# Moving the normed x 64 bytes along in SBUF, in a float32 decoder trunk on one core

## What is computed

```
h = rms_norm(x, pre_mix_norm[l])
proj = h @ w_in[l]                       # 2048 x 5648: q, k, v, z, xbc, dt
mix = concat(attention(q,k,v), ssd(xbc, dt, z))
x = x + rms_norm(mix @ w_out[l], post_mix_norm[l])          # 2048 x 2048
h = rms_norm(x, pre_mlp_norm[l])
x = x + rms_norm(square(relu(h @ w_up[l])) @ w_down[l], post_mlp_norm[l])   # 2048 x 8192, 8192 x 2048
```

## The kernel before, in words

| tile | first byte | its remainder by 128 |
|---|---|---|
| raw, w_hi, w_lo, x_sb | 16512, 32896, 49280, 65664 | 0 |
| a_hi, a_lo | 82048, 98432 | 0 |
| u_hi, u_lo, ybuf | 114816, 131200, 147584 | 0 |
| xbcT, x_tok, v_tok, zg, b_tok, convr | 163968 and on | 0 |
| wk, cbm | 206016, 214208 | 64 |
| wdt_both | 216256 | 64 |
| ident, tri, low | 218688, 219200, 219712 | 64 |

## Time and profile before

### The profile page before, as it was taken

One profiled execution on the slowest core, in us unless ns is written; L12 is line 12 of the kernel. 1 busy time (PEld: TensorE's weight loads), 2 busy tenths in 40 slices (PEclk: granted clock), 3 DMA queues, 4 the chain that ended last, 5 costly groups with the idle time before them and its releaser, 6 DMA issues.

```text
span 2248.1 us, 39497 instructions
## 1 busy us (share of the span) xinstructions
PE 2216.5 (99%) x14282; PEld 2023.7 (90%) x14282; DVE 1319.9 (59%) x1528; ACT 1016.3 (45%) x1280; POOL 109.9 (5%) x112
## 2 busy tenths in 40 slices
PE   8999999999999999999999999999999999999997
PEld 8999888998998998898899988889989989988986
DVE  6777465655555455555578775657554545554555
ACT  5443464543444344344454435545434434443443
POOL 2141000000000000000001410000000000000000
PEclk9999999999999999999999999999999999999999
DMA  6555556556656656655645555655666566556565
GB/s 204 152 170 157 161 188 198 177 179 200 189 180 192 190 179 193 190 184 187 193 125 166 166 161 151 198 185 182 190 192 186 173 201 188 184 189 193 176 194 163
DMA packets 208448, 406.21 MB, mean 181 GB/s; under 512 B 12540, under 2 KB 12820, under 8 KB 207828
## 3 DMA queue, kind: packets, MB, share of 16 engines
q1 hardware_dynamic: 206660, 398.04, 57.3%
q10 hardware_dynamic: 992, 4.78, 0.6%
q0 software_dynamic: 688, 1.90, 0.4%
HBM read 402.58 MB, written 2.10 MB: 180 GB/s over the span
## 4 chain that ended last, share of the span: by engine, by line
issue 71%; PE 26%; DVE 1%; ACT 0%; POOL 0%; DMA 0%; DVEq 0%; POOLq 0%; ACTq 0%
PE acc L734 5%; PE acc L737 5%; PE acc L736 5%; PE acc L699 3%; PE acc L701 3%; PE acc L700 3%; PE M L838 1%; PE M L751 1%; DVE x_sb L1111 0%; PE M L859 0%; DVE xbcT L1177 0%; DMA wk<-in_ssd_out_norm 0%; PE M L879 0%; POOL st L393 0%; DVE w_lo L1028 0%
## 5 line engine op out<-in xcount | busy, mean ns | idle before, releaser
L1028 DVE TENSOR_TENSOR w_lo<-raw,w_hi 128x1024 fp32r<-128x1024 f32 x755 | 927.7, 1235 | 793.4 <-ACT w_hi L462 790.1
L462 ACT ACTIVATE w_hi<-raw 128x1024 fp32r<-128x1024 f32 x755 | 794.5, 1058 | 1026.8 <-PE acc L701 521.6
L734 PE MATMUL acc<-a_hi,w_hi 128*128 128x256 f32 x2912 | 828.4, 284 | 1.8 <-DVE w_lo L1028 1.8
L736 PE MATMUL acc<-a_lo,w_hi 128*128 128x256 f32 x2912 | 823.9, 283 | 0.0
L737 PE MATMUL acc<-a_hi,w_lo 128*128 128x256 f32 x2912 | 823.9, 283 | 0.0
L734 PEld LDWEIGHTS acc<-a_hi,w_hi 128*128 128x128 f32 x2912 | 558.6, 192 | 4.1 <-DVE w_lo L1028 2.7
L736 PEld LDWEIGHTS acc<-a_lo,w_hi 128*128 128x128 f32 x2912 | 558.7, 192 | 1.8 <-issue 1.0
L737 PEld LDWEIGHTS acc<-a_hi,w_lo 128*128 128x128 f32 x2912 | 558.7, 192 | 0.0
L699 PE MATMUL acc<-w_hi,u_hi 128*128 128x512 f32 x1280 | 498.6, 390 | 0.0
L700 PE MATMUL acc<-w_lo,u_hi 128*128 128x512 f32 x1280 | 498.0, 389 | 0.0
L701 PE MATMUL acc<-w_hi,u_lo 128*128 128x512 f32 x1280 | 498.0, 389 | 0.0
(11 more groups left out here) (218 smaller groups left out, 1049.2 us busy)
## 6 DMA issues: line engine op xcount, KB each, us to landing
raw<-in_w_up SPq DMA_DIRECT2D x256, 512.0 KB, 3.7
raw<-in_w_down SPq DMA_DIRECT2D x256, 512.0 KB, 4.5
raw<-in_w_in SPq DMA_DIRECT2D x179, 512.0 KB, 3.8
raw<-in_w_out SPq DMA_DIRECT2D x64, 512.0 KB, 4.6
zg<-in_post_mix_norm ACTq DMA_DIRECT2D x2, 1024.0 KB, 4.6
zg<-in_post_mlp_norm ACTq DMA_DIRECT2D x2, 1024.0 KB, 6.4
out<-x_sb SPq DMA_DIRECT2D x8, 256.0 KB, 2.8
x_sb<-in_x POOLq DMA_DIRECT2D x3, 512.0 KB, 7.3
```

Of the source, the lines that this page charges most:

```text
L462: act.activation(w_hi[:, c % RING], raw[:, c % RING], ACT.Copy).then_inc(sem["hi_ready"], 1)
L734: pe.matmul(o(m), w(w_hi, kk, m), a_hi[:, k], start=(k == 0 and m % 2 == 0), stop=False, skip_group_check=True)
L736: pe.matmul(o(m), w(w_hi, kk, m), a_lo[:, k], start=False, stop=False, skip_group_check=True)
L1028: dve.tensor_tensor(w_lo[:, c % RING], raw[:, c % RING], w_hi[:, c % RING].bitcast(F32), ALU.subtract).then_inc(sem["split_done"], 1)
```

## The change

Two tiles of 64 bytes a partition, which nothing writes or reads, are declared ahead of `a_hi` and behind `a_lo`:

```diff
         x_sb = sb("x_sb", [P, TT, D])
+
+        sb("shift_a", [P, 16])
         a_hi = sb("a_hi", [P, KT, SEQ], F32R)
         a_lo = sb("a_lo", [P, KT, SEQ], F32R)
+        sb("shift_back", [P, 16])
         u_hi = sb("u_hi", [P, KT, SEQ], F32R)
         u_lo = sb("u_lo", [P, KT, SEQ], F32R)
```

## The result

| | before | changed |
|---|---|---|
| median of 5 runs each, us | 2249.82 (2249.32 to 2250.53) | 2258.80 (2258.25 to 2259.72) |
| ratio to before, with its 95% interval | | 1.0041 (1.0029 to 1.0054) |
| span of the profiled execution, us | 2248.1 | 2258.0 |
| forecast, us | | 2189 (2147 to 2220) |

The changed kernel is slower by 0.4%, some 9 us. The forecast was 61 us faster, and its range doesn't hold the result. In the changed kernel all lines behind the new declarations have moved on by 3: L734 is L737, L699 is L702, L1028 is L1031.

What follows compares the result with a forecast made beforehand. TensorE bounds the kernel: matmul count times the distance between starts. Gains of 57.3 (features) and 5.1 (v and z) less 0.4 (dt) and 1.0 (settling) make 61.0 us off 2248.1; with 1.7 us for the median, 2189 us, range 2147 to 2220.

Steps and rivals of the forecast that it cites:

- rival A: All matmuls: no change, the dt projection's 113.3 ns comes from something else; 2249.8 us, chance 12%.
- Rival D: Feature matmuls: slower, 126.7 ns, as the moving operand must begin on a multiple of 128; 2304 us, chance 8%.
- rival B: Feature, v and z matmuls: all of the excess goes, 109 ns, 11 less than now; 2147 us, chance 7%.
- Rival C: Half the gain, 3.3 ns on average: starts don't settle with operands changing between w_hi and w_lo; 2219 us, chance 7%.
- Everything behind them keeps its remainder by 128: Tiles behind the two new ones: the 3,840 matmuls with u stay at 226.7 ns, 0 us.
- the 24 starts are even to the 10 ns of the view: dt projection before: even starts over distances 64, 192, 320, 448 by 512, so only the remainder by 128 seems to matter.
- I take the dt projection's 113.3: Feature chunks, 256 columns: 113.3 ns instead of 120.0, 6.7 ns each, 57.3 us gained.
- My bounds of 109 and 126.7: Feature matmuls: 109 ns from x's transposes below, 126.7 above, as far over 120.0 as the dt projection is under.
- v and z: 768 matmuls of 512 columns, stationary a: the same 6.67 ns less each, 5.1 us gained.
- about 120: dt projection: its two operands now start alike, so 64 matmuls lose 6.67 ns each, 0.4 us.
- the 188 ns that I had named as a sign: Up projection: L734's weight loads at 188 ns in the median would show the forecast right.
- Settling: First few matmuls after other work, roughly 50 places a layer: some 2 us less gain at most, 1 taken.

Runs made afterwards that it cites:

- m1_offsets: Model left out, only TensorE works: 32 equal float32r matmuls per pair of operand offsets; 113.3 to 120.0 ns at 256 columns, 226.7 to 233.5 at 512.
- e2: Kernel before with only u, and all behind it, moved on by 128 bytes; 2272.04 us, ratio 1.0100.
- e1: Changed kernel with u 512 bytes behind its old place instead of 128; 2234.64 us, ratio 0.9934.
- e9: Changed kernel with u 256 bytes behind its old place instead of 128; 2234.76 us, ratio 0.9934.
- m2_grid: m1_offsets with all 64 offset pairs by 32 bytes and eight alternating patterns; distance 0 has 120.0 ns at 256 columns, 226.7 to 227.2 at 512.
- e7: Changed kernel with a moved by 192 bytes instead of 64, and u 256 bytes on; 2218.69 us, ratio 0.9861.
- e8: e7 with two float32 ident matmuls ahead of the first up block of each quarter from the second on; 2200.59 us, ratio 0.9781.
- e3: Kernel before with the weight ring (w_hi, w_lo) moved on by 64 bytes, a and u by 256; 2209.20 us, ratio 0.9820.
- e6: e1 with two float32 ident matmuls ahead of each pair of up blocks from the second quarter on; 2240.36 us, ratio 0.9957.
- e5: Kernel before with ring and u 64 bytes on by 256, plus two ident matmuls ahead of each pair of up blocks from the second quarter; 2216.25 us, ratio 0.9851.

## Why the prediction was wrong

It was right about what bounds the kernel. The time is the count of matmuls times their spacing, the waits stayed (0.1 us among the three of the earlier trace rows), no transfer and no split came late, and the place of the operands does alter the spacing: rival A's world, in which it can't matter, is excluded by m1_offsets. The Trainium skill, page "SBUF — State Buffer", section "Who interferes with whom", gives TensorE's moving operand and its weight load a read port each, independent of each other, and has it wait on no one. The small kernels, with no other engine at work, have 113.3 to 120.0 ns and 226.7 to 234.5 for the same shapes, by place. So the measurement decides against the conclusion that the place can't matter; whether the ports are what depends on each other, no run here shows.

Rival D put a slowdown on the features (126.7 ns), which in fact gained; rival B's 109 ns was seen at no distance. Rival C's small gain is near the 2.2 ns measured, but by another way: it blamed the change between tiles, and the small kernel has the 117.8 with one stationary and one moving tile. The 109 ns that B and D leaned on say little: the earlier trace rows are float32 transposes of 128 columns, not 256, and in the changed kernel, where ident's place turned their distance from +64 to -64, they start 109 ns apart as before. The slowdown came from where no rival looked. These steps failed:

- **"Everything behind them keeps its remainder by 128, so the 3,840 matmuls with u keep their 226.7 ns: 0 us."** They took 233.3 ns, +25 us, the largest term of all. u lies 128 behind its old place, and the period is 256: distance 128 costs 232.1 to 233.5 in the small kernels, e2 shows the loss alone, e1 and e9 undo it. Without it the change is 0.7% faster (e9, 2234.76).
- What it rested on: **"the 24 starts are even to the 10 ns of the view, so only the remainder by 128 seems to matter"**. By 256 the dt projection has distances 64 and 192 in turn, and each of them alone has another value, 113.3 and 117.8. The mix is even at 113.3, in m2_grid too. An even row over a mix doesn't show that its parts are alike.
- **"I take the dt projection's 113.3 ...; only which of the two is off the 128 differs."** It did matter which. The distance is +64 there in half of the matmuls, and -64 in all of the changed features: 117.8 instead of 113.3, a gain of 19.3 us instead of 57.3. But the sign is only a part of the 38 us between: with the other sign alone (e7) the features are at 117.18 on average, 13 us less than the change has. Another 20 us lie between e7 and e8 (114.93), in the state of the six long runs; the last 5 are short runs and first matmuls that stay above 113.3 in e8 too. My bounds of 109 and 126.7 held the 117.8.
- **v and z: "Since the excess was the same at both widths, I take the same 6.67 ns."** The size was nearly right and the sign wrong: +64 at 512 columns is 233.3, 6.6 more, and the term +4.0 us instead of -5.1.
- The dt projection, "about 120", came to 117.5 where its distances are now 128 and 0 in turn; it is worth 0.2 us. The weight loads came to the 188 ns that I had named as a sign, and yet the features didn't come to 113.3: the loads take 188 at 113.3 (e3) and at 117.8, so their length doesn't tell the one from the other. **"Settling"** was priced at 1 us, for the first few matmuls of each run. What stands ahead of a run can matter far more: two small matmuls ahead of each of six runs are the whole of the 18 us between e7 and e8.

By its own terms, the sum was -57.3 - 5.1 + 0.4 + 1.0 = -61.0; measured it was -19.3 + 4.0 + 25.2 + 0.2 = +10.1. Of the 71 us between them, 38 are the spacing at 256 columns, 25 the period, 9 the value at +64 with 512 columns; the rest, the dt projection's 0.2 and the 1.0 for settling, takes 1 off. The 8% for slower stood on rival D alone; the loss came from 3840 matmuls under a term put at nothing, and one row was all that put it there.

What stays open: why the distance acts as it does. That two reads of one memory meet in it is a guess; no run tests it. Whether a matmul's own weights or the next load's count is undecided by the patterns. Nor is it shown why there are two states at +64, what in an opening chooses between them, or why the changed kernel, e1, e6 and e9 have their short stretches at 113.3, at a distance of -64 where the small kernel never had them.

## What to carry to other kernels

Where a kernel is a row of float32r matmuls end to end, the start addresses of its operands are worth tuning. Here their difference counted by 256 bytes, with its sign, and apart for each width: measure a table of both widths in a small kernel first, and give each pair its own place. Padding ahead of one tile moves every tile behind it, so list all pairs that the move touches and price each one from a row at its new distance; "it stays aligned" is a claim about a period, and needs more than one row. And read a run's spacing at more than one place, for a state set at its head can hold through hundreds of matmuls.

## What the runs showed that I had not expected

- The best distance for 256 columns (+64: 113.3 ns against 120.0) is among the worst for 512 (233.3 against 226.7).
- At +64 and 256 columns there are two states, 113.3 and 117.8, that hold through runs of 768 matmuls, and behind two small matmuls either can turn into the other (e5). Twelve of them in the whole kernel are worth 18.1 us (2218.69 to 2200.59).
- A mix can be faster than its parts: stationary at 0 with moving at 0 and 64 in turn took 116.7 ns, where 0 has 120.0 and -64 has 117.8; distances of 64 and 192 in pairs took 113.3.
- Moving both operands together by 32 to 256 bytes from distance 0 changed nothing (120.0, 226.7 to 227.2). At other distances the difference is not the whole: the dt projection has 128 and 0 in turn both in the changed kernel and in e7, and takes 117.5 ns in the one and 120.0 in the other.
